# Gate and up products of a two-layer decoder: sixteen of 22 column pairs as seven quadrant products each (Strassen's method), x parked in DRAM meanwhile

## The chip, the cores and the metric

The kernel runs on one core of one Trainium2 chip. The metric is the device time of one execution in microseconds, as the median of three runs. A core has TensorE (PE, matrix products from SBUF into PSUM; the profile shows its weight loads as PEld), VectorE (DVE), ScalarE (ACT), GpSimd (POOL) and SyncE (SP, which issues most of the DMAs here). They run side by side and wait for each other through semaphores.

## The reference, cut to what matters

Two layers of a decoder, for 512 prompt tokens and 32 sample tokens (544 in all). Each layer ends with a gated feed-forward block; D_MODEL = 1024, D_FF = 2816, everything in float32.

```python
h2 = rms_norm(x, g_ffn[l])
gu = h2 @ w_gu[l]
x = x + (jax.nn.silu(gu[..., :D_FF]) * gu[..., D_FF:]) @ w_down[l]
```

Retention and block attention come before this in each layer; the change leaves them as they are.

## The kernel before

**Precision.** A matrix product in float32 is made of three products of rounded parts: each operand has a high part (a ScalarE copy to the type fp32r) and a low part (VectorE: the value minus its high part), and the sum is high x high + high x low + low x high. For weights these parts are WH and WL, for x after the norm's gain XH and XL, for the hidden layer AH and AL. Weights arrive in RAW, two slots of 2048 columns that take turns; each slot is split into WH (`L1072`, ScalarE) and WL (`L1436`, VectorE), and after that SP loads the next but one unit into the slot.

**Layout.** Features lie on the partitions: XT is 8 blocks of 128 features x 544 tokens, and a product's weights (128 x 128) are stationary while 272 tokens (half of 544) move. A *unit* f of the gate and up stage is 128 columns of the gate and the same 128 columns of up, 22 units per layer; a *tile* is one of the two, 8 blocks x 3 parts x 2 halves = 48 matmuls of 272 columns into two banks of PSUM. There are four such pairs of banks, and TensorE takes them in turn.

**One unit.** TensorE: `unit2`, two calls of `feature_tile` (`L637`). VectorE in `gu(i, j)`: multiplies the gate tile by the norm's factor RSTDB (`L1677`), ScalarE makes its sigmoid (`sig`, `L1273`), VectorE multiplies the two (`L1832`), scales the up tile (`L1677`), multiplies (`L1836`); ScalarE stores the high part of the result in AH (`L1335`), VectorE the low part in AL (`L1838`). The factor RSTDB is applied behind the product, so that the product can start before the norm is known.

**Start of the stage.** The first unit follows the output projection's last tile. VectorE adds each block of it to x (`residual`, `L1810`), ScalarE makes XH and the squares. TensorE sums the squares over the partitions (`square_sums`, `L532`), VectorE makes the variance, POOL the power -1/2 (`norm`, `L469`), VectorE puts it on diagonals (`L1382`), TensorE spreads these over all partitions (`spread`, `L542`) between the two tiles of unit 1, and VectorE copies the result into RSTDB (`L1387`, `L1388`). The fourth pair of banks, which unit 1's second tile uses, holds the spread values, so that tile waits for the copies (`rt_taken`).

**The order** is written out by hand: each engine has its own program, and semaphores count tiles (`tile_done`, `tile_free`), split units (`hi_ready`, `lo_ready`) and hidden tiles (`val_ready`, `hi_val`, `x_lo`). `hold` is a wait for a register's value, behind a wait that is always satisfied. After the stage comes the down projection: 8 tiles of 132 matmuls, whose results are added to x (`residual` again), after which the next layer starts.

## Time and profile before

| | us |
|---|---|
| median of 3 runs (lowest, highest) | 2082.14 (2081.86, 2082.91) |
| the profiled execution, its own time | 2080.78 |
| its span, first to last instruction | 2079.2 |
| TensorE busy in the span | 2032.4 |
| VectorE busy | 973.1 |
| ScalarE busy | 685.0 |
| POOL busy | 127.5 |
| mean granted TensorE clock, as a share of full speed | 0.997 |

The profiled execution is one run under the hardware profiler. Busy time is the union of an engine's instructions; matmuls overlap in it (each is shown with 288 ns, though one starts every 125), so their number times their duration says nothing, and the distance between starts does. The chain that ended last is followed back from the last instruction to whatever released it.

### The profile page before, as it was taken

The numbers are of one execution on the slowest core, as the hardware profiler recorded it, in microseconds if no ns is written. First come the engines' busy times: TensorE is split into PE (matmuls) and PEld (weight loads), VectorE is DVE, ScalarE is ACT, GpSimd is POOL, SyncE is SP. The second block draws the span as 40 slices with busy tenths as digits, with TensorE's granted clock in tenths as the row PEclk, the third lists the DMA queues.
The fourth block names the chain that finished last, engine by engine and source line by source line (L and its number), as shares of the span: only waits on it lengthen the run. The fifth ranks groups of instructions, "written<-read, shape, count | busy, mean of one in ns | idle before, by whom it ended". The sixth has DMA issues, their size and how long they took to land.

```text
span 2079.2 us, 45110 instructions
## 1 busy us (share of the span) xinstructions
PE 2032.4 (98%) x17393; PEld 1909.0 (92%) x17393; DVE 973.1 (47%) x1620; ACT 685.0 (33%) x1054; POOL 127.5 (6%) x211
## 2 busy tenths in 40 slices
PE   7989999999999999999999899999999999999999
PEld 6968978989999999999998698799899999999998
...
GB/s 194 123 44 207 214 276 114 86 139 162 120 100 82 83 99 81 82 72 94 96 150 125 65 216 231 273 52 92 198 117 110 106 82 81 83 99 68 84 83 91
DMA packets 257967, 253.20 MB, mean 122 GB/s; under 512 B 12266, under 2 KB 223378, under 8 KB 257554
## 3 DMA queue, kind: packets, MB, share of 16 engines
...
q14 instruction: 62, 0.51, 0.1%
q10 hardware_dynamic: 128, 0.15, 0.0%
...
## 4 chain that ended last, share of the span: by engine, by line
PE 94%; DVE 2%; ACT 2%; issue 1%; DMA 1%; ACTq 0%; POOLq 0%; DVEq 0%; POOL 0%
PE PS L637 62%; PE PS L618 3%; PE PS L793 3%; PE PS L619 3%; PE PS L620 3%; PE PS L598 2%; PE PS L599 2%; PE PS L600 2%; PE PS L804 2%; PE PS L851 1%; PE PS L577 1%; PE PS L733 1%; PE PS L749 1%; ACT PT L1153 1%; PE PS L670 1%
## 5 line engine op out<-in xcount | busy, mean ns | idle before, releaser
L637 PE MATMUL PS<-XH,WH 128*128 128x272 f32 x2176 | 454.6, 290 | 5.1 <-DVE EA L1728 3.2
L637 PE MATMUL PS<-XH,WL 128*128 128x272 f32 x2176 | 450.4, 288 | 0.0
L637 PE MATMUL PS<-XL,WH 128*128 128x272 f32 x2176 | 448.7, 288 | 0.0
L1436 DVE TENSOR_TENSOR WL<-RAW,WH 128x2048 fp32r<-128x2048 f32 (+2 forms) x144 | 310.7, 2157 | 227.1 <-ACT WH L1072 226.3
L637 PEld LDWEIGHTS PS<-XH,WH 128*128 128x128 f32 x2176 | 342.0, 188 | 12.6 <-DVE EA L1728 8.2
L637 PEld LDWEIGHTS PS<-XL,WH 128*128 128x128 f32 x2176 | 341.9, 188 | 0.0
L637 PEld LDWEIGHTS PS<-XH,WL 128*128 128x128 f32 x2176 | 339.9, 189 | 0.0
L1072 ACT ACTIVATE WH<-RAW 128x2048 fp32r<-128x2048 f32 (+2 forms) x152 | 274.5, 1806 | 94.7 <-PE PS L637 87.9
L1677 DVE TENSOR_TENSOR EA<-PS,RSTDB 128x544 f32<-128x544 f32 x120 | 86.3, 721 | 226.5 <-PE PS L637 225.8
L1273 ACT ACTIVATE EB<-EA 128x544 f32<-128x544 f32 x92 | 60.5, 658 | 327.9 <-DVE EA L1677 274.2
L618 PE MATMUL PS<-WH,XH 128*128 128x256 f32 x512 | 153.2, 299 | 0.0
L637 PE MATMUL PS<-AH,WH 128*128 128x272 f32 x704 | 146.1, 289 | 0.0
L619 PE MATMUL PS<-WL,XH 128*128 128x256 f32 x512 | 145.3, 284 | 0.0
L637 PE MATMUL PS<-AL,WH 128*128 128x272 f32 x704 | 145.2, 287 | 0.0
L637 PE MATMUL PS<-AH,WL 128*128 128x272 f32 x704 | 145.0, 287 | 0.0
L620 PE MATMUL PS<-WH,XL 128*128 128x256 f32 x512 | 144.5, 282 | 0.0
L598 PE MATMUL PS<-WH,XH 128*128 128x256 f32 x384 | 110.4, 287 | 8.8 <-DVE WL L1423 6.7
L618 PEld LDWEIGHTS PS<-WH,XH 128*128 128x128 f32 x512 | 97.6, 191 | 21.6 <-ACT RV L1085 12.6
L637 PEld LDWEIGHTS PS<-AL,WH 128*128 128x128 f32 x704 | 111.0, 188 | 0.0
L637 PEld LDWEIGHTS PS<-AH,WL 128*128 128x128 f32 x704 | 109.9, 188 | 0.0
L637 PEld LDWEIGHTS PS<-AH,WH 128*128 128x128 f32 x704 | 109.9, 188 | 0.0
L599 PE MATMUL PS<-WL,XH 128*128 128x256 f32 x384 | 109.4, 285 | 0.0
...
## 6 DMA issues: line engine op xcount, KB each, us to landing
...
```

The source lines that it names most:

```text
L598: pe.matmul(out, a, wh[:, k], start=k == 0, stop=False)
L599: pe.matmul(out, a, wl[:, k], start=False, stop=False)
L600: last = pe.matmul(out, b, wh[:, k], start=False, stop=k == KT - 1)
L618: pe.matmul(out, a, wh[:, k], start=k == 0, stop=False)
L619: pe.matmul(out, a, wl[:, k], start=False, stop=False)
L620: last = pe.matmul(out, b, wh[:, k], start=False, stop=k == KT - 1)
L637: last = pe.matmul(PS[:, 2 * pair + h, 0:HALF], w[:, i, c0:c0 + P], x[:, k, h * HALF:(h + 1) * HALF], start=first and i == 0 and a == 0, s ...
L793: last = pe.transpose(PS[:, (c + 2) % 3, hp * P:(hp + 1) * P], buf[:, b, hp * P:(hp + 1) * P], IDENT)
L1072: act.activation(WH[:, slot, 0:n], RAW[:, slot, 0:n], ACT.Copy).then_inc(hi_ready, 1)
L1273: act.activation(EB[:, dst, :], EA[:, src, :], ACT.Sigmoid).then_inc(sig_done, 1)
L1436: dve.tensor_tensor(WL[:, slot, 0:n], RAW[:, slot, 0:n], WH[:, slot, 0:n].bitcast(F32), ALU.subtract).then_inc(lo_ready, 1)
L1677: dve.tensor_tensor(halves(dst), pair[p], RB, ALU.mult).then_inc(tile_free, 1)
```

## The change

**The quadrants.** For units 6 to 21 (NC = 6), x after norm and gain (8 blocks x 544 tokens) is cut into four quadrants of 4 blocks x 272 tokens, and a unit's weights into four quadrants of 4 blocks x 128 columns: 11 and 21 are the two halves of the gate's blocks, 12 and 22 those of up. The product of two 2 x 2 matrices is then made of seven products of quadrants (or of sums of them) in place of eight. A quadrant product is 4 blocks x 3 parts = 12 matmuls of 272 columns.

**x.** ScalarE writes x times its gain into XF (8 operations), VectorE multiplies it by RSTDB, makes four sums of quadrants (SF), and the two split the four sums and three plain quadrants (Q11, QS1, QS2, Q12, QS3, QS4, Q22) into high and low parts. QS1 and QS2 lie where XT is, so POOL first stores XT to DRAM (`x_parked`, 2.2 MB) and loads it back after the last unit. Q12, QS3, QS4 and Q22 lie where XH and XL are, which units 0 to 5 read.

**The weights.** RAW's slot holds four quadrants, from four DMAs of 256 KB in place of two of 512 KB. For each unit the three quadrants 11, 21 and 22 are split as they are (`a_high`, `a_low`, 1536 columns), VectorE makes four sums in place (`w_sums`, 512 columns each, each waiting for the one before), and four sums are split in two pairs (`t12_*`, `t34_*`, 1024 columns each). The parts lie in CH, over WH and WL.

**The products.** Three PSUM banks per unit, two sets for odd and even units. The first product goes into bank a; ScalarE copies it to bank c, where the fourth is added; the second goes to bank f and is copied to one more bank; third, fifth and seventh are added to a, the sixth to f, and ScalarE copies a twice to SBUF in between. One extra matmul marks bank c as written, so that the fourth product adds to ScalarE's copy. VectorE's `up_sum`, `gate_mul` and `gated_up` make the hidden tile, and the bank set is free after `gate_mul`.

**Other parts.** `spread` is moved from behind unit 1's first tile to behind its fifth block of eight. The hidden layer's last blocks lie in a tail. A wait for x's return is added to the down projection's residual.

```diff
+    QUAD = 8 * HK * HALF
+    Q11 = quadrant_pair("Q11", TAILOFF)
+    QS1, QS2 = quadrant_pair("QS1", 16512), quadrant_pair("QS2", 16512 + QUAD)
+    Q12, QS3, QS4, Q22 = (quadrant_pair(n, XHOFF + i * QUAD) for i, n in enumerate(("Q12", "QS3", "QS4", "Q22")))
+    XF = at("XF", [P, KT, N], F32, R0 + 12 * N * 4)
...
+    XTF = nc.dram_tensor("x_parked", [P, KT, N], F32)
...
+            hold(pool, x_lo, lay * NX + X0["out"] + KT)
+            hold(pool, xg_done, lay + 1)
+            pool.dma_start(XTF.ap(), XT[:]).then_inc(xf_kept, 16)
             norm(2 * lay + 2)
+            hold(pool, tile_done, lay * NT + T0["down"])
+            hold(pool, xf_kept, lay * 16 + 16)
+            pool.dma_start(XT[:], XTF.ap()).then_inc(xf_back, 16)
...
-            feature_tile(T0["gu"] + 2, 2, 1, UC, 0, kk, x)
+            feature_tile(T0["gu"] + 2, 2, 1, UC, 0, kk, x, final=False, part=kk[:5])
             spread(2 * lay + 2, (6, 7))
+            feature_tile(T0["gu"] + 2, 2, 1, UC, 0, kk, x, first=False, part=kk[5:])
...
+            def seven(f, j):
+                at_c, s = w_chunks(j), f - NC
+                c_bank, a_bank, f_bank = 4 * j, 4 * j + 1, 4 * j + 2
+                a_hi, a_lo = CH[:, a_slots(j, 0)], CH[:, a_slots(j, 1)]
+                t1, t2 = (0, 1) if j else (1, 0)
...
+                def product(q, w, bank, n, start=False):
+                    if isinstance(f, int) and f == NC:
+                        pe.wait_ge(q_lo, lay * 7 + n)
+                    wh, wl = (v.rearrange("p (k c) -> p k c", c=P) for v in w)
+                    for k in range(HK):
+                        for m, (a, b) in enumerate(((wh, q[0]), (wh, q[1]), (wl, q[0]))):
+                            last = pe.matmul(PS[:, bank, 0:HALF], a[:, k, :], b[:, k, :],
+                                             start=start and k == m == 0, stop=k == HK - 1 and m == 2,
+                                             skip_group_check=not start)
+                    return last
+                def copies(n):
+                    pe.wait_ge(copied, lay * (4 * NSU) + 4 * s + n)
+                pe.wait_ge(la_ready, lay * NSU + s + 1)
+                pe.wait_ge(tile_free, lay * NT + 2 * f + T0["gu"])
+                if isinstance(f, int) and f == NC:
+                    pe.wait_ge(q_lo, lay * 7 + 1)
+                pe.matmul(PS[:, c_bank, 0:HALF], a_hi[:, at_c["11"] - 1, 0:P], Q11[0][:, 0, :], start=True, stop=True)
+                product(Q11, a_chunk("11"), a_bank, 1, start=True).then_inc(prod, 1)
+                pe.wait_ge(l12_ready, lay * NSU + s + 1)
+                product(QS1, t_chunk(t12, t1), f_bank, 2, start=True).then_inc(prod, 1)
+                copies(1)
+                product(QS2, t_chunk(t12, t2), a_bank, 3).then_inc(prod, 1)
+                product(Q12, a_chunk("21"), c_bank, 4).then_inc(prod, 1)
+                pe.wait_ge(lo_ready, lay * NU + f + (U0["gu"] + 3))
+                copies(3)
+                product(QS3, t_chunk(t34, 0), a_bank, 5).then_inc(prod, 1)
+                product(QS4, a_chunk("22"), f_bank, 6).then_inc(prod, 1)
+                copies(4)
+                product(Q22, t_chunk(t34, 1), a_bank, 7).then_inc(tile_done, 2)
+            seven(NC, 0)
+            seven(NC + 1, 1)
+            with pe.Fori(NC // 2 + 1, FT // 2) as i:
+                for j in range(2):
+                    seven(2 * i + j, j)
...
+            def a_high(f, j):
+                s = f - NC
+                hold(act, landed[j], (lay * NU + U0["gu"] + f) * 16 + (32 - 16 * j))
+                hold(act, landed_up[j], (lay * NSU + s) * 16 + (32 - 16 * j))
+                if isinstance(f, int) and f == NC:
+                    unit_done(NC - 2)
+                else:
+                    act.wait_ge(prod, lay * (6 * NSU) + 6 * (s - 1) + 1)
+                act.activation(CH[:, a_slots(j, 0)], raw_chunks(j)[:, 1:4], ACT.Copy).then_inc(ha_ready, 1)
...
+            def seven(f, j):
+                b = 4 * j
+                first = isinstance(f, int) and f == NC
+                if first:
+                    unit_done(NC - 1)
+                    quad_hi(4, Q12, x_quad(XF, 1, 0))
+                    quad_hi(5, QS3, SF[:, 2])
+                else:
+                    gate_high(f - 1, 1 - j)
+                    t34_high(f, j)
+                copy(f, PS[:, b, 0:HALF], b + 1, 1)
+                if first:
+                    quad_hi(6, QS4, SF[:, 3])
+                    quad_hi(7, Q22, x_quad(XF, 1, 1))
+                elif isinstance(f, int) and f == FT - 1:
+                    split(U0["down"], 0, 11 * P, (prod, lay * (6 * NSU) + 6 * (f - NC) + 1))
+                else:
+                    a_high(f + 1, 1 - j)
+                copy(f, PS[:, b + 3, 0:HALF], b + 2, 2)
+                if not first:
+                    hidden_high(f - 1)
+                copy(f, EB[:, 1, 0:HALF], b + 1, 3)
+                if first:
+                    sig(T0["gu"] + 2 * (NC - 1), 0, 0, 0)
+                copy(f, EB[:, 1, HALF:N], b + 1, 5)
+                if first:
+                    hidden_high(NC - 1)
+                    a_high(f + 1, 1 - j)
+                if not (isinstance(f, int) and f == FT - 1):
+                    t12_high(f + 1, 1 - j)
...
             ahead("gu", 0, 0, 2)
+            for k in range(KT):
+                xg = act.activation(XF[:, k, :], XT[:, k, :], ACT.Copy,
+                                    scale=GT[:, bass.ds(8 * lay + (k + 16), 1)])
+            xg.then_inc(xg_done, 1)
             ahead("gu", 0, 1, 2)
             gu(0, 0)
+            ahead("gu", 1, 0, 2)
             gu(0, 1)
-            with act.Fori(1, FT // 2) as i:
+            quad_hi(1, Q11, x_quad(XF, 0, 0))
+            ahead("gu", 1, 1, 2)
+            gu(1, 0)
+            act.wait_ge(xf_kept, lay * 16 + 16)
+            quad_hi(2, QS1, SF[:, 0])
+            ahead("gu", 2, 0, 2)
+            gu(1, 1)
+            quad_hi(3, QS2, SF[:, 1])
+            a_high(NC, 0)
+            gu(2, 0)
+            t12_high(NC, 0)
+            t34_high(NC, 0)
+            seven(NC, 0)
...
+            def quad_low(n, q, src):
+                dve.wait_ge(q_hi, lay * 7 + n)
+                dve.tensor_tensor(q[1][:], src, q[0][:].bitcast(F32), ALU.subtract).then_inc(q_lo, 1)
+            def a_low(f, j):
+                dve.wait_ge(ha_ready, lay * NSU + (f - NC) + 1)
+                dve.tensor_tensor(CH[:, a_slots(j, 1)], raw_chunks(j)[:, 1:4], CH[:, a_slots(j, 0)].bitcast(F32),
+                                  ALU.subtract).then_inc(la_ready, 1)
+            def w_sums(f, j):
+                r, c, n = raw_chunks(j), w_chunks(j), lay * (4 * NSU) + 4 * (f - NC)
+                b11, b12, b21, b22 = (r[:, c[q], :] for q in ("11", "12", "21", "22"))
+                dve.wait_ge(la_ready, lay * NSU + (f - NC) + 1)
+                dve.tensor_tensor(b11, b11, b12, ALU.subtract).then_inc(w_sum, 1)
+                dve.wait_ge(w_sum, n + 1)
+                dve.tensor_tensor(b12, b22, b12, ALU.subtract).then_inc(w_sum, 1)
+                dve.wait_ge(w_sum, n + 2)
+                dve.tensor_tensor(b22, b22, b11, ALU.add).then_inc(w_sum, 1)
+                dve.wait_ge(w_sum, n + 3)
+                dve.tensor_tensor(b21, b21, b22, ALU.subtract).then_inc(w_sum, 1)
+            def t12_low(f, j):
+                dve.wait_ge(h12_ready, lay * NSU + (f - NC) + 1)
+                dve.tensor_tensor(t12(f, 1), raw_t12(j), t12(f, 0).bitcast(F32), ALU.subtract).then_inc(l12_ready, 1)
+            def t34_low(f, j):
+                dve.wait_ge(hi_ready, lay * NU + f + (U0["gu"] + 1))
+                dve.tensor_tensor(t34(f, 1), raw_t34(j), t34(f, 0).bitcast(F32), ALU.subtract).then_inc(lo_ready, 1)
+            def up_sum(f, j):
+                s = f - NC
+                dve.wait_ge(prod, lay * (6 * NSU) + 6 * s + 6)
+                dve.wait_ge(copied, lay * (4 * NSU) + 4 * s + 4)
+                if isinstance(f, int) and f == FT - 1:
+                    dve.wait_ge(x_lo, lay * NX + X0["gu"] + f)
+                dve.tensor_tensor(halves(EA[:, 1, :]), halves(EB[:, 1, :]), pair[2 * j + 1], ALU.subtract)
+            def gate_mul(f, j):
+                dve.wait_ge(sig_done, lay * NSIG + f + (S0N["gu"] + 1))
+                dve.tensor_tensor(halves(EB[:, 0, :]), pair[2 * j], halves(EB[:, 0, :]), ALU.mult).then_inc(tile_free, 2)
+            def gated_up(f):
+                dve.wait_ge(tile_free, lay * NT + 2 * f + (T0["gu"] + 4))
+                dve.tensor_tensor(EA[:, 1, :], EA[:, 1, :], EB[:, 0, :], ALU.mult).then_inc(val_ready, 1)
+            def seven(f, j):
+                last = isinstance(f, int) and f == FT - 1
+                up_sum(f - 1, 1 - j)
+                gate_mul(f - 1, 1 - j)
+                t34_low(f, j)
+                gated_up(f - 1)
+                if last:
+                    split(U0["down"], 0, 11 * P)
+                else:
+                    a_low(f + 1, 1 - j)
+                hidden_low(f - 1)
+                if not last:
+                    w_sums(f + 1, 1 - j)
+                    t12_low(f + 1, 1 - j)
...
+            split(U0["gu"] + 1, 1, 8 * UC)
             variance(2 * lay + 2, 6)
             spread_rt(2 * lay + 2)
-            ahead("gu", 0, 1)
+            split(U0["gu"] + 2, 0, 8 * UC)
             take_rt(2 * lay + 2, (6, 7))
             dve.wait_ge(rt_taken, 2 * lay + 2)
-            gu(0, 0)
-            gu(0, 1)
-            hold(dve, tile_free, lay * NT + T0["gu"] + 4)
-            with own.loop(FT // 2 - 1, 2) as i:
+            gu(0)
+            dve.wait_ge(xg_done, lay + 1)
+            dve.tensor_tensor(XF[:], XF[:], RSTDB[:].unsqueeze(1).to_broadcast([P, KT, N]), ALU.mult)\
+                .then_inc(xf_ready, 1)
+            split(U0["gu"] + 3, 1, 8 * UC)
+            gu(1)
+            dve.wait_ge(xf_ready, lay + 1)
+            quad_sum(SF[:, 0], xa(1, 0), xa(1, 1), ALU.add)
+            quad_sum(SF[:, 2], xa(0, 0), xa(1, 0), ALU.subtract)
+            dve.wait_ge(sf_ready, lay * 4 + 1)
+            quad_sum(SF[:, 1], SF[:, 0], xa(0, 0), ALU.subtract)
+            quad_low(1, Q11, xa(0, 0))
+            split(U0["gu"] + 4, 0, 8 * UC)
+            gu(2)
+            dve.wait_ge(sf_ready, lay * 4 + 3)
+            quad_sum(SF[:, 3], SF[:, 1], xa(0, 1), ALU.subtract)
+            quad_low(2, QS1, SF[:, 0])
+            split(U0["gu"] + 5, 1, 8 * UC)
+            gu(3)
+            quad_low(3, QS2, SF[:, 1])
+            a_low(NC, 0)
+            gu(4)
+            w_sums(NC, 0)
+            t12_low(NC, 0)
+            t34_low(NC, 0)
+            quad_low(4, Q12, xa(0, 1))
+            quad_low(5, QS3, SF[:, 2])
+            quad_low(6, QS4, SF[:, 3])
+            quad_low(7, Q22, xa(1, 1))
+            gu(NC - 1)
+            a_low(NC + 1, 1)
+            w_sums(NC + 1, 1)
+            t12_low(NC + 1, 1)
+            seven(NC + 1, 1)
```

**How the order of instructions moves.** VectorE in the loop over the units, register rows left out: before, one unit (EA and EB are the scaled tiles in SBUF, PS is PSUM):

```order
L1436 TENSOR_TENSOR WL<-RAW,WH 128x2048
L1677 TENSOR_TENSOR EA<-PS,RSTDB 128x544
L1832 TENSOR_TENSOR EB<-EB,EA 128x544
L1677 TENSOR_TENSOR EA<-PS,RSTDB 128x544
L1836 TENSOR_TENSOR EA<-EA,EB 128x544
L1838 TENSOR_TENSOR AL<-EA,AH 128x544
```

and after the change, one unit (RAW<-RAW are the four sums; CH<- the low parts of the weights; T34H holds the high parts of T3 and T4):

```order
L2124 TENSOR_TENSOR EA<-EB,PS 128x544
L2128 TENSOR_TENSOR EB<-PS,EB 128x544
L2115 TENSOR_TENSOR CH<-RAW,T34H 128x2x512
L2132 TENSOR_TENSOR EA<-EA,EB 128x544
L2093 TENSOR_TENSOR CH<-RAW,CH 128x1536
L2082 TENSOR_TENSOR AL<-EA,AH 128x544
L2101 TENSOR_TENSOR RAW<-RAW 128x512
L2103 TENSOR_TENSOR RAW<-RAW 128x512
L2105 TENSOR_TENSOR RAW<-RAW 128x512
L2107 TENSOR_TENSOR RAW<-RAW 128x512
L2111 TENSOR_TENSOR CH<-RAW,CH 128x1024
```

The two scalings by RSTDB and the split of 2048 columns are gone; in their place there are two operations on PSUM, low parts of 1024, 1536 and 1024 columns and four sums of 512.

VectorE between unit 5 and unit 7 (units 6's low parts, four quadrants of x, all of unit 5, and the low part of unit 7's plain quadrants):

```order
L2115 TENSOR_TENSOR FIRST34L<-RAW,FIRST34H 128x1024
L2089 TENSOR_TENSOR Q12L<-XF,Q12H 128x1088
L2089 TENSOR_TENSOR QS3L<-SF,QS3H 128x1088
L2089 TENSOR_TENSOR QS4L<-SF,QS4H 128x1088
L2089 TENSOR_TENSOR Q22L<-XF,Q22H 128x1088
L1917 TENSOR_TENSOR EA<-PS,RSTDB 128x544
L2069 TENSOR_TENSOR EB<-EB,EA 128x544
L1917 TENSOR_TENSOR EA<-PS,RSTDB 128x544
L2073 TENSOR_TENSOR EA<-EA,EB 128x544
L2082 TENSOR_TENSOR AL<-EA,AH 128x544
L2093 TENSOR_TENSOR CH<-RAW,CH 128x1536
```

The four low parts of x stand ahead of unit 5's products with PSUM, and `CH<-RAW,CH 128x1536`, which unit 7's first product waits for, behind all of them.

TensorE around the spread in unit 1 (EA holds the diagonals, REGISTER_ALU prepares the wait at the head of a tile), before: the last rows of the unit's first tile, the spread, the head of its second:

```order
L637 MATMUL PS<-XH,WH 128x272 x2
L637 MATMUL PS<-XL,WH 128x272 x2
L637 MATMUL PS<-XH,WL 128x272 x2
L542 MATMUL PS<-EA,FIX 128x128 x4
L543 MATMUL PS<-EA,FIX 128x32
L631 REGISTER_ALU
L637 MATMUL PS<-XH,WH 128x272 x2
L637 MATMUL PS<-XL,WH 128x272 x2
L637 MATMUL PS<-XH,WL 128x272 x2
L637 MATMUL PS<-XH,WH 128x272 x2
```

and after the change, from the spread on:

```order
L623 MATMUL PS<-EA,FIX 128x128 x4
L624 MATMUL PS<-EA,FIX 128x32
L719 MATMUL PS<-XH,WH 128x272 x2
L719 MATMUL PS<-XL,WH 128x272 x2
L719 MATMUL PS<-XH,WL 128x272 x2
L719 MATMUL PS<-XH,WH 128x272 x2
L719 MATMUL PS<-XL,WH 128x272 x2
L719 MATMUL PS<-XH,WL 128x272 x2
L719 MATMUL PS<-XH,WH 128x272 x2
L719 MATMUL PS<-XL,WH 128x272 x2
L719 MATMUL PS<-XH,WL 128x272 x2
L712 REGISTER_ALU
```

Nine rows of the first tile, 18 matmuls, now stand behind the spread and ahead of the second tile.

## Rows read from the trace of the kernel before

**Rows 1.** The page: busy time by engine, and the chain by engine.
```profile
PE 2032.4 (98%) x17393; PEld 1909.0 (92%) x17393; DVE 973.1 (47%) x1620; ACT 685.0 (33%) x1054; POOL 127.5 (6%) x211
...
PE 94%; DVE 2%; ACT 2%; issue 1%; DMA 1%; ACTq 0%; POOLq 0%; DVEq 0%; POOL 0%
```

**Rows 2.** The chain in order of time, one entry (start, us, what).
```profile
664.66 379.43 PE PS L637 x3024
```

**Rows 3.** Timeline of one gate and up unit: start us, us, engine, operation.
```profile
759.33 2.29 DVE L1436 TENSOR_TENSOR WL<-RAW,WH 128x2048 fp32r<-128x2048 f32 x1 [0.96 <-ACT WH L1072]
...
759.97 0.41 PE L637 MATMUL PS<-XH,WL 128*128 128x272 f32 x2
...
760.22 0.41 PE L637 MATMUL PS<-XH,WH 128*128 128x272 f32 x2
...
761.54 0.72 DVE L1677 TENSOR_TENSOR EA<-PS,RSTDB 128x544 f32<-128x544 f32 x1
...
762.29 0.66 ACT L1273 ACTIVATE EB<-EA 128x544 f32<-128x544 f32 x1 [2.99 <-DVE EA L1677]
...
767.19 0.72 DVE L1677 TENSOR_TENSOR EA<-PS,RSTDB 128x544 f32<-128x544 f32 x1 [3.48 <-PE PS L637]
...
767.95 0.72 DVE L1836 TENSOR_TENSOR EA<-EA,EB 128x544 f32<-128x544 f32 x1
...
768.87 0.66 ACT L1335 ACTIVATE AH<-EA 128x544 f32 x1 [5.92 <-DVE EA L1836]
```

**Rows 4.** Timeline at the start and the end of the gate and up stage.
```profile
643.10 0.41 PE L637 MATMUL PS<-XH,WH 128*128 128x272 f32 x2
...
655.33 1.91 ACT L1072 ACTIVATE WH<-RAW 128x2048 fp32r<-128x2048 f32 x1 [7.73 <-PE PS L637]
...
656.63 1.20 POOL L469 TENSOR_TENSOR SM<-SM 128x5 f32<-128x5 f32 x1 [56.41 <-DVE SM L1377]
...
662.32 0.94 PE L542 MATMUL PS<-EA,FIX 128*128 128x128 f32 x7
...
911.31 0.41 PE L637 MATMUL PS<-AH,WH 128*128 128x272 f32 x2
```

**Rows 5.** Timeline: TensorE behind a wait that ended late, in the gate stage.
```profile
460.73 0.52 PE L637 MATMUL PS<-XH,WH 128*128 128x272 f32 x2 [0.51 <-DVE EA L1728]
```

**Rows 6.** VectorE by form: names, shapes, count | busy us, mean ns | idle before.
```profile
L1436 DVE TENSOR_TENSOR WL<-RAW,WH 128x2048 fp32r<-128x2048 f32 x120 | 274.9, 2291 | 220.0 <-ACT WH L1072 220.0
...
L1442 DVE TENSOR_TENSOR WL<-RAW,WH 128x1024 fp32r<-128x1024 f32 x16 | 19.5, 1221 | 15.0 <-ACT WH L1072 15.0
...
L1795 DVE TENSOR_TENSOR G<-G,EA 128x544 f32 x12 | 8.7, 726 | 2.8 <-DVE EA L1791 2.8
...
L1648 DVE TENSOR_TENSOR RK<-RK,CL 128x512 f32<-128x512 f32 x8 | 5.0, 684 | 0.0
```

**Rows 7.** ScalarE by form, the same columns.
```profile
L1072 ACT ACTIVATE WH<-RAW 128x2048 fp32r<-128x2048 f32 x128 | 244.3, 1908 | 94.7 <-PE PS L637 87.9 <-DMA RAW<-in_w_in 6.7
...
L1040 ACT ACTIVATE XH<-XT,GT x32 | 24.0, 751 | 181.4 <-DVE XT L1810 181.4
...
L1072 ACT ACTIVATE WH<-RAW 128x1024 fp32r<-128x1024 f32 x8 | 8.4, 1051 | 0.0
...
L1153 ACT ACTIVATE PT<-PS 128x256 f32<-128x256 f32 x8 | 3.1, 384 | 5.2 <-PE PS L733 5.2
```

**Rows 8.** The weight DMA's line, 700 to 900 us: duration ns min/median/max; landing.
```profile
L382 SPq DMA_DIRECT2D RAW<-in_w_gu x30: 372/383/396, 701.8 to 870.7; - x30
...
DMA to landing us min/median/max: 3.1/4.0/5.1
```

**Rows 9.** DMA issues of the whole span: KB each, median us to landing.
```profile
x_kept<-XT SPq DMA_DIRECT2D x2, 2048.0 KB, 10.9
```

**Rows 10.** Two windows: busy us of each engine, granted clock, DMA share, GB/s.
```profile
20.00:30.00 10.00, 6.11 (x41) 6.09 (x42) 6.25 (x12) 8.33 (x11) 0.00 (x0) 0.66 0.09 15
1040.00:1050.00 10.00, 7.97 (x71) 7.73 (x71) 2.20 (x4) 1.30 (x2) 0.00 (x0) 1.00 0.47 138
```

140 lines of the change are left out of this document (122 added, 18 removed).

## The prediction

> **What bounds the kernel now.** The page's first part says that TensorE is busy for 98% of the span, and the chain that ended last is TensorE for 94% [rows 1]. Both only say where to look, since a busy TensorE may still wait inside a stage. The chain in order of time settles it for this stage: one stretch of 3024 matmuls without another engine in it, 379.43 us, from the second tile of unit 1 through the gate and up products and all of the down projection [rows 2]. That is 0.1255 us per matmul, tile boundaries and loop branches included. So here a matmul that is removed is worth its pitch, as long as nothing else becomes late. The timeline of one unit shows the pitch and how idle the others are: two matmuls every 0.25 us, while VectorE has six operations and ScalarE three in a unit of 12.03 us (the greater part of them in [rows 3]). From the first matmul of the stage to the first of the down projection it is 911.31 - 643.10 = 268.2 us [rows 4], and twice that in the program.
>
> **TensorE's part.** A unit (128 gate and 128 up columns) costs 2 tiles x 8 x 3 x 2 = 96 matmuls of 272 columns. Unit 2 starts at 664.66 + 48 x 0.1254 = 670.68, and twenty units later it is 911.31: 12.03 us each [rows 2, 4]. As seven products it is 7 x 4 x 3 = 84 and one that only marks a bank: 85, of the same width and with one weight load each, as before. 12.03 x 85/96 = 10.65, plus 0.01 for each of seven boundaries (the 0.1255 above against 0.1253 inside a tile, over 48 matmuls): 10.72 us, 1.31 less. Sixteen units give **-21.0 us** per layer. Bounds: no boundary cost, 10.65; or a restart at every product as after the wait at 460.73, whose pair took 0.52 in place of 0.41 [rows 5], 7 x 0.11 more, 11.4. I take the low side, since the wait of that row came late and these come long before.
>
> The Trainium skill (TensorE: Matmul & The Clock Gate, section on the back-to-back issue gap) gives columns/2.4 + 2.5 ns for a lone stream, 116 ns for 272 columns. By it the eleven matmuls are worth 1.27 us a unit and not 1.38; the rows say 125, and the measurement decides.
>
> **Does VectorE keep up?** Its chain for one unit in the new loop, with durations from [rows 3, 6]: two operations on PSUM 2 x 0.72, low part of T3/T4 (1024) 1.22, product 0.72, low part of the three plain quadrants (1536, between 1024 and 2048) 1.76, low part of the hidden tile 0.72, four sums of 512 at 0.68, low part of T1/T2 1.22: 9.8 us. An independent operation starts 0.08 before the one ahead ends (759.33 + 2.29 against 761.54), one that waits for its predecessor 0.04 after (767.19 + 0.72 against 767.95) [rows 3]; seven of the first and three of the second, -0.4. After the third sum ScalarE needs 1.05 for the high part, of which the fourth sum covers 0.7: +0.4. About **9.8 to 9.9 us per unit against 10.72**: VectorE goes from half busy to 90%, but does not bound. ScalarE: 0.66 sigmoid, 1.05, 1.48, 1.05 for the splits, 0.66 hidden, four copies of 272 at 0.40 = 6.5 us [rows 3, 7].
>
> Where in the unit are the waits (t = 0 its first matmul)? Product 1 ends at 1.6, and then every 1.5. ScalarE sees the unit before finished at 0.2, sigmoid to 0.9, T3/T4 high to 1.8, first copy about 2.2; product 3 needs it at 3.1. VectorE: gate product 0.9 to 1.6, T3/T4 low to 3.1; product 5 needs it at 6.2. T1/T2 low of the next unit is finished at 9.8 to 10, needed at 12.3. Slack everywhere is 0.9 us or more, so the steady loop should run at TensorE's pace. The landing: a slot of RAW is free at 3.1, now four issues of 0.38 and about 4.0 to land (5.1 at most) [rows 8], so 5.5 to 6.7; ScalarE reads it 9.9 us after it was free. 3 us of cover.
>
> **The first six units.** New beside them: on ScalarE eight products of 0.75 [rows 7] (in a hole of 7.7 us before 655.33 [rows 4]), three high parts of 1088; on VectorE 4352 elements (4.7 by the same slope), four sums and three low parts of 1088 at 1.29. A unit's own work is 2.29 + 5 x 0.72 = 5.9 us of VectorE and leaves 6.1: the new 13.7 us fit into the 30 of five units, and counted through in order the low parts of the weights of units 3, 4 and 5 are still finished 7 us before TensorE asks. Zero; if the cover went, at most the 4.7 would show once. POOL has the store of x ahead of its power for the norm: a DMA issue took 0.38 on SP [rows 8], and ScalarE is done at about 653, 3.6 us before the power starts at 656.63 [rows 4]. Zero, or 1 at most.
> **Spread moved.** Tile 2 of unit 1 now has its last 18 matmuls (2.3 us) behind the broadcast of the norm. Now TensorE waits from the broadcast at 662.32, which takes about 1.2, until 664.66 [rows 2, 4]: **-1.1 us**.
>
> **The change of regime, units 6 and 7.** Here I expect the loss. T=0 is unit 6's start. Four quadrants of x live where XH and XL were, so their low parts can only follow unit 5: VectorE has T3/T4 low until 2.3, four low parts of 1.29 until 7.2, and only then unit 5's own five operations with ScalarE's two between (7.1 to 10.7). ScalarE makes unit 5's hidden high part until 11.5 and, behind it in its queue, the high part of unit 7's quadrants until 12.9; VectorE's low part ends at 14.7. TensorE could have started unit 7 at 10.85 and starts at 14.8: **+4.0**. Then three sums (2.2), ScalarE 1.05, VectorE 1.22: 19.3, where product 2 wants it at 16.4: **+2.9**. Product 3 of unit 6 waits 0.1 for its copy. Bounds: 6.5 if every handover is as short as 0.03 (762.29 behind 761.54 + 0.72), 8.5 if each is the 0.20 of 768.87 behind 767.95 + 0.72 [rows 3].
> **The end.** The old loop freed each bank pair in the unit's middle; now both are freed together after the sigmoid, and the first down tile asks for that: 0.2 + 0.66 + 0.72 and handovers, **+1.8** (bounds 1.6 and 2.1). Today there is nothing there: 911.31 follows the last gate matmul. The way back of x (2.2 MB; a 2 MB store took 10.9 [rows 9], so some 12 to 14 us with the issue) is asked for 18 us later, by the first residual: hidden.
>
> **Sum per layer:** -21.0 - 1.1 + 7.0 + 1.8 = -13.3; twice, -26.7. The profiled execution took 2080.78 us around a span of 2079.2; the median of the three is 2082.14, 1.36 more. 2080.8 - 26.7 = 2054.1, and on the median's scale **2055 us**.
>
> **Rivals.**
> *A, the clock falls after the stall.* TensorE is idle 4.0 us, works 1.6, is idle 2.9. With 2.0 of 10 us not busy the granted clock stayed at 1.00 from 1040 to 1050; with 3.9 of 10 it was 0.66 from 20 to 30, so partly at 1.2 and partly at 2.4 GHz [rows 10]. Around unit 7 it is 6.9 in some 10 us. Price: 0.34 of 10 us is 3.4 us lost, so up to 3.4 per layer: 2062. The Trainium skill (TensorE: Matmul & The Clock Gate, section on why this matters) states that an idle gap between bursts throttles the engine again; by this rule A is what happens. The rows agree for the longer pause and not for the short one.
> *B, VectorE sets the pace mildly.* If half of its junctions cost more than I gave them, the chain is 11.2 us and not 9.9. Then 14 units lose 0.45 each: +6.3 per layer, 2068. For: 90% load and no run of such a chain in the trace. Against: 0.85 us of margin.
> *C, slower.* One mechanism: the waits in VectorE's chain. Where a hold on its own semaphore stood before the sum of L1795 it was idle for 2.8/12 = 0.23 us [rows 6]. Eleven such junctions in each unit make 9.8 + 2.5 = 12.4 us. From 11.7 on the sixteen units are no gain (13.3/14 = 0.95 above 10.72); at 12.4 it is +1.7 x 14 - 13.3 = +10 per layer, **2102 us**. Against it: the chain's waits are of the kind of L1836 (0.04), without the hold.
> *D, the change doesn't do what it says.* Every product restarts TensorE (11.4 us a unit, above): 0.7 x 16 = 11 per layer come back, 2078, a gain that can hardly be measured.
>
> **Numbers.** Forecast 0.60; A 0.14; B 0.16; C 0.05; D 0.05. Forecast's own bounds: 2055 less 2 (boundaries), less 1 (short handovers) and plus 3 (long ones), 2052 to 2058. A and B take the top to 2068, and below I leave 3 more, since unit 7's loss is a sum of fourteen steps that may overlap more than I see: 2049 to 2068, which leaves out C, D and the upper part of B. A measurement of this kernel can tell 0.2%, 4 us, from no change. Faster by more: forecast, A, B and half of D, 0.92; within: 0.03; slower: 0.05.
>
> **What would show it.** In the new profile: units of unit 8 on 10.7 us apart, with no idle time of TensorE inside; VectorE at 90% in that stretch and its waits for TensorE and the sigmoid still there (if they are gone, B or C); TensorE idle near 4 and 3 us at the first and second product of unit 7 and 1.8 before the first down matmul; granted clock behind unit 7 (A); first pairs of products at 0.41 and not 0.52 (D). The forecast is wrong if the steady period is above 11, or if unit 7 loses less than 5 or more than 9 us.

## Result and the profile of the changed kernel

The changed kernel takes **2056.88 us** (median of 4 runs, 2053.70 to 2059.82) against 2082.0 us before (4 runs beside it): ratio 0.9879, 95% interval 0.9862 to 0.9896. The forecast was 2055 us, in the range 2049 to 2068. The profiled execution took 2053.70 us around a span of 2052.1, 27.1 less than the 2079.2 of before; the sum of the prediction said 26.7.

The page's first part, busy time and instructions of each engine, answers to [rows 1]:

```profile
PE 1996.7 (97%) x17041; PEld 1870.4 (91%) x17041; DVE 1124.9 (55%) x1804; ACT 805.8 (39%) x1276; POOL 130.8 (6%) x215
```

TensorE has 352 matmuls and 35.7 us of busy time less; the span lost only 27. The chain of layer 1 and the same marks of layer 2, in order of time (start, length, what), answers to [rows 2, 4]. An entry that follows another without a wait begins where that one ends:

```profile
654.71 0.79 PE PS L613 x8
...
655.67 3.97 PE PS L719 x30
...
660.86 44.46 PE PS L719 x354
...
728.10 1.48 ACT CH L1490
729.61 1.77 DVE CH L2093
...
733.57 1.07 ACT CH L1498
734.66 1.23 DVE CH L2111
735.94 9.35 PE PS L1114 x72
745.29 0.12 PE PS L1126
745.42 10.56 PE PS L1114 x84
...
756.10 10.57 PE PS L1114 x84
...
766.79 10.57 PE PS L1114 x84
...
884.42 10.58 PE PS L1114 x84
...
895.03 0.63 ACT EB L1515
...
895.75 0.73 DVE EB L2128
...
896.53 132.37 PE PS L719 x1056
...
1666.96 44.46 PE PS L719 x354
...
1742.05 10.69 PE PS L1114 x72
...
1903.98 132.39 PE PS L719 x1056
```

Where before one stretch of TensorE ran through, there is now a piece of ScalarE and VectorE at unit 7 (728 to 736), then unit after unit at 10.69 us (884.42 - 745.42 = 139.00 for thirteen), then 1.53 us without a matmul before down (896.53 - 884.42 - 10.58), in which ScalarE makes unit 21's sigmoid and VectorE its `gate_mul`.

A matmul is shown with 0.29 us although the next one starts after 0.125. So what a wait costs is read from starts. From the timeline of TensorE (start, length, what): the first matmul of units 6, 7 and 8, the last of unit 21, the first of down:

```profile
717.14 0.29 PE L1126 MATMUL PS<-Q11H,CH 128*128 128x272 f32 x1
...
731.49 0.59 PE L1126 MATMUL PS<-Q11H,CH 128*128 128x272 f32 x1 [3.53 <-DVE CH L2093]
...
745.13 0.29 PE L1126 MATMUL PS<-Q11H,CH 128*128 128x272 f32 x1
...
894.70 0.29 PE L1114 MATMUL PS<-Q22H,CH 128*128 128x272 f32 x1
...
896.53 0.51 PE L719 MATMUL PS<-AH,WH 128*128 128x272 f32 x2 [1.54 <-DVE EB L2128]
```

Units 6 and 7 took 745.13 - 717.14 = 27.99 us, 6.6 more than two of 10.69. The first matmul of down started 1.83 us after the last of unit 21, so the junction cost 1.7. What TensorE waits for, over the whole program (us in total, times, longest):

```profile
PE PS L1126 <- DVE CH L2093: 7.1, 2, 3.5
...
PE PS L719 <- DVE EB L2128: 3.1, 2, 1.5
PE PS L1114 <- DVE CH L2111: 2.8, 2, 1.7
```

The columns of the next view are busy time (with the number of instructions) of TensorE, of its weight loads, VectorE, ScalarE and POOL, then granted clock, DMA share and GB/s. Three stretches: layer 1's unit 7, the steady units of layer 1, layer 2's unit 7:

```profile
728.00:732.00 4.00, 0.51 (x2) 0.51 (x3) 3.09 (x3) 1.57 (x2) 0.00 (x0) 0.92 0.00 0
732.00:736.00 4.00, 2.86 (x14) 2.54 (x12) 3.50 (x6) 2.43 (x4) 0.00 (x0) 0.65 0.00 0
736.00:740.00 4.00, 4.00 (x32) 4.00 (x33) 4.00 (x5) 3.09 (x6) 0.00 (x0) 1.00 0.04 13
...
745.00:884.00 139.00, 139.00 (x1107) 139.00 (x1106) 124.25 (x145) 80.27 (x117) 0.00 (x0) 1.00 0.33 96
...
1736.00:1740.00 4.00, 2.40 (x13) 2.41 (x13) 3.86 (x5) 0.32 (x1) 0.00 (x0) 0.79 0.00 0
1740.00:1744.00 4.00, 2.30 (x10) 1.98 (x10) 3.60 (x5) 3.88 (x5) 0.00 (x0) 0.50 0.00 0
1744.00:1748.00 4.00, 4.00 (x30) 4.00 (x29) 3.97 (x6) 1.35 (x3) 0.00 (x0) 0.86 0.52 152
```

In the steady stretch TensorE is never idle and VectorE is busy 89%. What VectorE still waits for there, in one unit of its timeline, is ScalarE, four times and 1.05 us together:

```profile
797.32 1.23 DVE L2111 TENSOR_TENSOR CH<-RAW,CH 128x1024 fp32r<-128x1024 f32 x1 [0.40 <-ACT CH L1498]
...
799.52 0.72 DVE L2128 TENSOR_TENSOR EB<-PS,EB 128x544 f32<-128x544 f32 x1 [0.35 <-ACT EB L1515]
800.40 1.23 DVE L2115 TENSOR_TENSOR CH<-RAW,T34H 128x1024 fp32r<-128x1024 f32 x1 [0.15 <-ACT T34H L1506]
...
802.41 1.76 DVE L2093 TENSOR_TENSOR CH<-RAW,CH 128x1536 fp32r<-128x1536 f32 x1 [0.15 <-ACT CH L1490]
```

At unit 7 the clock falls in both layers, in layer 1 only while product 1 runs, in layer 2 until 1744 and later. The chain shows what that costs: the same 72 matmuls take 9.35 us in layer 1 and 10.69 in layer 2.

**A measure for the experiments.** From the first matmul behind the spread to the first of down it is 896.53 - 660.86 = 235.67 us in layer 1 and 1903.98 - 1666.96 = 237.02 in layer 2. Where the clock holds, such "stage times" come again to 0.01 us in other kernels of the same order, while the run times scatter by 5 us and more; so what a few us mean is read from them. (What comes before the stage ends at different times in the profiles, 653.5 to 657.5; the kernel before, at 655.3, lies among them.)

### The profile page after: what moved, and what is told of

The parts are those of the page before. It is cut to its first block, busy times and chain, and to the rows that moved or that the text cites. A ratio compares the mean times of both kernels' runs of the same rounds, so it can differ in the third digit from the quotient of the medians.

```text
span 2052.1 us, 45522 instructions
## 1 busy us (share of the span) xinstructions
PE 1996.7 (97%) x17041; PEld 1870.4 (91%) x17041; DVE 1124.9 (55%) x1804; ACT 805.8 (39%) x1276; POOL 130.8 (6%) x215
## 4 chain that ended last, share of the span: by engine, by line
PE 90%; DVE 4%; ACT 3%; issue 2%; DMA 1%; ACTq 0%; DVEq 0%; POOLq 0%; POOL 0%
PE PS L719 43%; PE PS L1114 15%; PE PS L699 3%; PE PS L700 3%; PE PS L701 3%; PE PS L875 3%; PE PS L679 2%; PE PS L680 2%; PE PS L681 2%; PE PS L933 2%; PE PS L886 1%; PE PS L658 1%; PE PS L815 1%; PE PS L831 1%; ACT PT L1287 1%
## 5 line engine op out<-in xcount | busy, mean ns | idle before, releaser
L1676 DVE TENSOR_TENSOR WL<-RAW,WH 128x2048 fp32r<-128x2048 f32 (+2 forms) x112 | 236.0, 2107 | 198.5 <-ACT WH L1206 197.6
L1206 ACT ACTIVATE WH<-RAW 128x2048 fp32r<-128x2048 f32 (+2 forms) x120 | 212.5, 1771 | 106.0 <-PE PS L719 95.4
L719 PE MATMUL PS<-XH,WH 128*128 128x272 f32 x1152 | 243.1, 292 | 3.2 <-DVE EA L1968 3.2
L719 PE MATMUL PS<-XL,WH 128*128 128x272 f32 x1152 | 237.9, 288 | 0.0
L719 PE MATMUL PS<-XH,WL 128*128 128x272 f32 x1152 | 237.7, 288 | 0.0
L719 PEld LDWEIGHTS PS<-XH,WH 128*128 128x128 f32 x1152 | 180.6, 188 | 10.6 <-DVE EA L1968 8.2
L719 PEld LDWEIGHTS PS<-XL,WH 128*128 128x128 f32 x1152 | 181.0, 188 | 0.0
L719 PEld LDWEIGHTS PS<-XH,WL 128*128 128x128 f32 x1152 | 180.3, 189 | 0.0
L701 PE MATMUL PS<-WH,XL 128*128 128x256 f32 x512 | 144.1, 281 | 0.0
L1407 ACT ACTIVATE EB<-EA 128x544 f32<-128x544 f32 x60 | 39.5, 660 | 228.2 <-DVE EA L1917 174.4
L699 PEld LDWEIGHTS PS<-WH,XH 128*128 128x128 f32 x512 | 97.1, 190 | 21.6 <-ACT RV L1219 11.7
L681 PE MATMUL PS<-WH,XL 128*128 128x256 f32 x384 | 109.3, 285 | 0.0
```

The source lines that it names most:

```text
L681: last = pe.matmul(out, b, wh[:, k], start=False, stop=k == KT - 1)
L699: pe.matmul(out, a, wh[:, k], start=k == 0, stop=False)
L701: last = pe.matmul(out, b, wh[:, k], start=False, stop=k == KT - 1)
L719: last = pe.matmul(PS[:, 2 * pair + h, 0:HALF], w[:, i, c0:c0 + P], block[:, h * HALF:(h + 1) * HALF], start=first and i == 0 and a == 0, ...
L1206: act.activation(WH[:, slot, 0:n], RAW[:, slot, 0:n], ACT.Copy).then_inc(hi_ready, 1)
L1676: dve.tensor_tensor(WL[:, slot, 0:n], RAW[:, slot, 0:n], WH[:, slot, 0:n].bitcast(F32), ALU.subtract).then_inc(lo_ready, 1)
```

## Experiments

Ten kernels, and the changed one again, in three groups; each group ran on one chip beside the kernel before. Ratios are to the kernel before.

**1. TensorE kept busy in unit 7's waits.**

```diff
...
+                if isinstance(f, int) and f == NC + 1:
+                    pe.wait_ge(tile_free, lay * NT + 2 * f + T0["gu"])
+                idle_work(26)
                 pe.wait_ge(la_ready, lay * NSU + s + 1)
...
                 product(Q11, a_chunk("11"), a_bank, 1, start=True).then_inc(prod, 1)
+                idle_work(20)
```

> The changed kernel, with 26 and then 20 matmuls whose result nobody reads, issued by TensorE into the free bank 7 where it waits at unit 7 (before its product 1 and before its product 2). Nothing of the result is left out. My theory: both waits stay where they are, since VectorE ends them; TensorE only looks busy in them. What changes is the clock behind them: in the changed kernel's trace the last 72 products of unit 7 took 9.35 us in layer 1 and 10.69 us in layer 2, against 72 x 125.3 ns = 9.02 us at full clock. With the clock kept at 1.00 this gives back 0.33 + 1.67 = 2.0 us of the profiled run, and more in the runs that lay up to 6 us over it: the median should come to 2052 to 2054 us, and the four to six runs should lie within 2 us of one another in place of 6. The rival (the scatter has nothing to do with unit 7's clock) expects the same scatter and a time of 2055 to 2059 us. A second rival: the added matmuls end too late and delay product 1, then the time rises by up to 2 us for both layers.

2052.84 us (4 runs, 2049.83 to 2054.92), ratio 0.9856 (0.9841 to 0.9871). The stage takes 235.67 us in both layers, and the 72 matmuls behind the wait 9.34 in both. The windows over the same place as above:

```profile
728.00:732.00 4.00, 4.00 (x34) 4.00 (x33) 2.53 (x4) 2.04 (x2) 0.00 (x0) 1.00 0.00 0
732.00:736.00 4.00, 3.81 (x31) 3.59 (x30) 3.60 (x5) 0.96 (x1) 0.00 (x0) 1.00 0.00 0
736.00:740.00 4.00, 3.86 (x31) 3.64 (x30) 3.86 (x5) 3.61 (x6) 0.00 (x0) 1.00 0.01 4
```

VectorE is no earlier, so nothing but the clock changed: its fall cost 0 in layer 1 and 1.35 us in layer 2 of the changed kernel's profile, not 2.0. My expectation had counted 72 x 125.3 ns = 9.02 us; they take 9.34 at full clock too, since the entry counts the last matmul to its end (0.16) and the first behind a wait takes 0.1 longer. The fall costs nothing where it is over by the end of product 1, since product 2 waits for VectorE anyway. The granted clock over the whole run rose to 0.997 to 0.999. The scatter of 5 us did not shrink to the 2 us I had expected, so unit 7's clock is not what makes most of it.

**2. Without the matmul that marks bank c.**

```diff
-                pe.matmul(PS[:, c_bank, 0:HALF], a_hi[:, at_c["11"] - 1, 0:P], Q11[0][:, 0, :], start=True, stop=True)
```

> The changed kernel without the one matmul per unit whose result product 2 overwrites. What is computed stays the same. If TensorE alone sets the pace of the sixteen units, each becomes shorter by one matmul, 10.69 to 10.56 us, and the time falls by 32 x 0.125 = 4.0 us (2052 to 2054 us). The rival, that VectorE's chain (9.8 us of work in 10.69) or the slots it frees set the pace in part, expects less than half of that, 0 to -2 us, and idle time of TensorE inside the units.

(The matmul's result is overwritten by ScalarE's copy, not by product 2 as the expectation says.) 2050.14 us (5 runs, 2047.35 to 2052.65), ratio 0.9845 (0.9832 to 0.9859). Layer 1's stage takes 233.94 us, 1.73 less: that is 14 matmuls of 0.125, those of units 8 to 21. Those of units 6 and 7 are worth nothing, since there TensorE only comes earlier to a wait that VectorE ends. In layer 2 the clock fell for longer, and the stage took 235.91. So TensorE alone sets the pace of the steady units. (Why the fourth product needs no mark to add to ScalarE's copy here, no run shows.)

**3, 4. Three, and one, more VectorE operations per unit.**

```diff
                 gated_up(f - 1)
+                for i in range(3):
+                    dve.tensor_reduce(SM[:, 76 + 2 * i:78 + 2 * i] if i < 2 else SM[:, 90:92], PADSRC, AX, ALU.max)
```

> The changed kernel with three operations of VectorE more in each of the units 7 to 21: each reduces 512 elements of a constant to two numbers that nobody reads. Each should take 0.55 to 0.75 us, so VectorE's work rises from 8.9 us busy of a 10.69 us unit to about 10.8 us, over the pace of TensorE with the waits between the operations (9.8 us with them before). My theory (VectorE has about 0.9 us of room) expects the unit at 10.69 + 0.6 to 1.6 us, 11.3 to 12.3 us, TensorE waiting within each unit, and 15 x 2 x that = +18 to +48 us. If a wait of TensorE in each unit also pulls the clock down, products take up to twice as long and the time rises far more, by over 100 us. If VectorE had more room than I thought (its waits shrink by what is added), the rise is below 10 us.

Three: 2075.45 us (6 runs, 2073.33 to 2077.47), ratio 0.9971 (0.9959 to 0.9983). The stage takes 247.27 us, 11.60 more, which is 0.83 for each of fourteen units: 11.52 us per unit. Twelve units of it, first by group of instructions (busy us, mean ns | idle before, releaser), then as a window:

```profile
L2144 DVE TENSOR_REDUCE SM<-FIX 128x2 f32<-128x512 f32 x36 | 22.4, 677 | 0.0
L1114 PE MATMUL PS<-QS1H,CH 128*128 128x272 f32 x96 | 21.3, 302 | 6.7 <-DVE CH L2111 6.7
L1114 PEld LDWEIGHTS PS<-QS1H,CH 128*128 128x128 f32 x96 | 15.8, 188 | 9.4 <-DVE CH L2111 9.4
```

```profile
753.00:891.00 138.00, 131.26 (x1021) 128.62 (x1020) 131.97 (x169) 70.83 (x108) 0.00 (x0) 1.00 0.32 91
```

The chain shows VectorE's three operations as 1.78 us on the path of every unit, and TensorE waits once in each, at product 2, for the low part of T1 and T2. VectorE's own timeline has only one wait left in a unit, the 0.40 us for ScalarE. So VectorE needs 11.52 - 1.78 = 9.74 us for a unit without them: 0.95 of room. The wait of each unit, 0.56 us of matmuls and 0.78 of weight loads (6.7 and 9.4 in twelve units), did not lower the clock: it is 1.00 in the window.

> The changed kernel with one operation of VectorE more in each of the units 7 to 21, of 0.60 us (three of them took 1.78 us in the kernel with three, whose units became 11.52 us long, 0.83 us over TensorE's pace). By the same count one of them leaves VectorE's chain at 11.52 - 1.19 = 10.33 us, under TensorE's 10.69: the unit stays at 10.69 us, its only cost is at unit 7, where VectorE is already late, so 2 x 0.6 us at most, +1 us. The rival, that every addition of VectorE's is paid in part even under the pace (a third of 0.6 us per unit), expects +6 us.

One: 2054.47 us (4 runs, 2048.73 to 2056.69), ratio 0.9868 (0.9849 to 0.9886). The stage takes 235.66 us in both layers, unchanged to 0.01. VectorE under TensorE's pace costs nothing (9.74 + 0.59 against 10.69); over it, the excess is paid in full.

**5. x parked twice.**

```diff
             pool.dma_start(XTF.ap(), XT[:]).then_inc(xf_kept, 16)
+            pool.dma_start(XTF2.ap(), XT[:]).then_inc(xf_kept, 16)
...
-            hold(pool, xf_kept, lay * 16 + 16)
+            hold(pool, xf_kept, lay * 32 + 32)
             pool.dma_start(XT[:], XTF.ap()).then_inc(xf_back, 16)
+            hold(pool, xf_back, lay * 32 + 16)
+            pool.dma_start(XT[:], XTF2.ap()).then_inc(xf_back, 16)
```

> The changed kernel with x stored to DRAM twice and brought back twice, one after the other: 2176 KB more each way and layer, the second store holding back ScalarE's first write to the place of x, the second load the first addition of x at the down tiles. My theory prices the parking at nothing: the store takes 7.6 us from issue to landing and is over long before QS1 is written, the way back is hidden behind the wait for the first down tile. Twice as much should then cost 0 to 1 us per layer, 0 to 2 us in all; the second load ends some 8 to 10 us later than the first, which still lies within the first two down tiles (2 x 2.75 us do not quite hold it), so VectorE's first addition may be late by up to 4 us, and TensorE has four banks of slack before it waits. The rival, that the parking takes bandwidth from the weight loads of the first units or holds back ScalarE, expects +3 us or more, the same amount that the parking itself costs now.

2054.93 us (4 runs, 2053.01 to 2057.85), ratio 0.9872 (0.9857 to 0.9887): no dearer than once. The second way back was late for VectorE in one layer, and TensorE, with its banks ahead, had no wait for it:

```profile
DVE XT L2054 <- DMA XT<-x_parked: 5.8, 1, 5.8
```

Layer 2's stage is 235.67 us. Layer 1's is 237.79, where the 72 matmuls of unit 7 took 11.45 us, 2.11 more than at full clock: again the clock and nothing else. The parking is free, and a transfer twice as long would be.

**6. The order before unit 7 changed** (VectorE; ScalarE's queue is changed to match).

```diff
+            scaled(tile, 2, EA[:, 0, :])
+            a_low(NC + 1, 1)
             quad_low(6, QS4, SF[:, 3])
+            dve.wait_ge(sig_done, lay * NSIG + g + (S0N["gu"] + 1))
+            own.mark(dve.tensor_tensor(EB[:, 0, :], EB[:, 0, :], EA[:, 0, :], ALU.mult))
             quad_low(7, Q22, xa(1, 1))
-            gu(NC - 1)
-            a_low(NC + 1, 1)
+            scaled(tile + 1, 3, EA[:, 1, :])
...
             w_sums(NC + 1, 1)
+            hidden_low(g)
             t12_low(NC + 1, 1)
```

> The changed kernel with VectorE's and ScalarE's work before unit 7 in another order: the residues and high parts of unit 7's own weights (a_high, a_low) are taken before the last two quadrants' (quad_hi and quad_low 6 and 7), and these are put between the steps of unit 5's gate. Nothing is left out. In the changed kernel TensorE waits 3.5 us before unit 7's product 1 for VectorE's a_low and 1.2 to 1.7 us before product 2 for t12_low, with product 1 at the half clock between them: 28 matmuls in 2 to 3 us less or more. Stepping through the order with the measured durations, a_low is ready before TensorE comes, so the first wait goes and what is left of the second is 1 to 2 us; unit 8 starts about 3 us earlier in each layer: -6 us, 2050 to 2051 us. The clock should then also fall less behind it. The rival (VectorE is late as a whole, its work before unit 8 cannot be moved but only added up) expects that the wait moves to product 2 or to unit 8 with the same length, and the time stays within 1 us of the changed kernel's.

2048.91 us (5 runs, 2045.48 to 2049.82), ratio 0.9841 (0.9828 to 0.9855). TensorE's waits in layer 1 from 700 to 760:

```profile
PE PS L1114 <- DVE CH L2111: 2.5, 1, 2.5
```

The wait before product 1 is gone, the one before product 2 is 2.5 us, and the stage takes 232.62 us, 3.05 less. VectorE now works without a pause from 717.8 to 733.9, so what is left is its amount of work and not its order. In layer 2 the clock fell behind the one wait too: 234.13, 1.51 more.

**7. The first down tile waits for its own bank only.** `feature_tile` begins with `pe.wait_ge(tile_free, lay * NT + tile + 3 - depth)`.

```diff
                         last = feature_tile(tile, m, j, P, 0, range(11 * j, 11 * j + 11), (HIDDEN_HI, HIDDEN_LO), j == 0, j == 1,
-                                            depth=2)
+                                            depth=4 if isinstance(i, int) and m == 0 else 2)
```

> The changed kernel, whose first down tile takes its chunks with a look-ahead of four matmul groups in place of two, so that TensorE reaches the last hidden chunk (k = 21, the one that unit 21's gate gives) later within its tile. Nothing is left out. TensorE waits 1.5 us at the start of down for the unit 21's sigmoid and VectorE's product in both layers. My theory: the wait is for work that ends about 1.5 us after unit 21's last product, so doing as much other work first hides it: -1.5 us a layer, -3 us in all (2053 to 2054 us). The rival: the wait is not for the hidden chunk but for a bank that VectorE's gate_mul frees, then the look-ahead changes nothing and the 1.5 us stay.

2054.46 us (4 runs, 2050.42 to 2054.92), ratio 0.9865 (0.9850 to 0.9880). The wait is gone: down begins at once behind unit 21.

```profile
887.64 10.57 PE PS L1114 x84
898.21 16.89 PE PS L719 x135
```

(For this the first round of the loop over the down tiles is written out, which the diff above does not show.) The expectation reads `depth` as a look-ahead over the chunks, and the order of the matmuls is in fact the same as before. `depth` says how many tiles back the bank must have been freed. With 2, the first down tile waits for `gate_mul` of unit 21; with 4, for that of unit 20. Unit 20 is the last that used the banks 0 and 1, into which this tile writes; unit 21 lies in 4 to 7. So the run shows the very thing that the expectation's rival names: the wait was for a freed bank, as the prediction has it, and for the bank of the wrong unit.

In this profile the clock cost 2.28 and 1.98 us at unit 7 (72 matmuls in 11.62 and 11.32 us), so the stage reads 236.41 and 236.09: without it 234.1, which is 235.67 - 1.53. (By starts the gain is 1.7, since the entry at 898.21 begins 0.17 after its first matmul.) Read from the run times alone the edit would have looked like nothing.

**8. Only the spread moved, in the kernel before.**

```diff
-            feature_tile(T0["gu"] + 2, 2, 1, UC, 0, kk, x)
+            feature_tile(T0["gu"] + 2, 2, 1, UC, 0, kk, x, final=False, part=kk[:5])
             spread(2 * lay + 2, (6, 7))
+            feature_tile(T0["gu"] + 2, 2, 1, UC, 0, kk, x, first=False, part=kk[5:])
```

> The kernel before, with only the place of the spread (the two small products that turn the root-mean-square into a row of factors) moved as in the change: before the last three chunks of unit 0's third tile in place of behind it. The parts of the change that make seven products of eight are not in it. My theory: VectorE's copy of the factors then runs beside the three chunks' matmuls, the wait of 1.3 us behind the spread goes, and each layer becomes 1.1 us shorter: -2.2 us against the kernel before, 2079 to 2080.5 us. The rival, that the gate's first use of the factors is the one that is waited for, expects no change.

2078.01 us (11 runs, 2075.35 to 2080.64), ratio 0.9983 (0.9974 to 0.9992). From the sums of squares to the entry behind the spread the chain has 660.15 - 654.00 = 6.15 us; before it was 664.66 - 655.29 = 9.37, in which TensorE did 18 matmuls more (2.26 us). That is 0.96 us per layer, and 1.03 by the starts of the matmuls. It is not all that the edit gave. From the first square sum to the first matmul of down, by the timelines:

```profile
655.13 0.95 PE L532 MATMUL PS<-FIX,EB 128*128 128x1 f32 x8
...
911.31 0.41 PE L637 MATMUL PS<-AH,WH 128*128 128x272 f32 x2
```

```profile
653.84 0.83 PE L532 MATMUL PS<-FIX,EB 128*128 128x1 f32 x7
...
908.43 0.41 PE L637 MATMUL PS<-AH,WH 128*128 128x272 f32 x2
```

256.18 us before, 254.59 in this kernel: 1.59 less per layer, 3.2 in the program, well inside the interval (0.8 to 2.6 per thousand, 1.7 to 5.4 us). The other 0.55 are spread over the stage: a unit takes 12.00 us and not 12.03, and no run shows why. In the changed kernel units 2 to 5 take 12.00 us too. The 1.0 us per layer of the spread, and the 0.1 of these first units, have nothing to do with the seven products.

**9. The three gains together, without and with filling the wait; and the changed kernel again.**

> The changed kernel with the new order before unit 7, the deeper look-ahead of the first down tile, and without the matmul that marks bank c. From the first matmul behind the spread to the first of down, the profiles without a fall of the clock took 235.67 us; the order alone took 232.62 (-3.05), the look-ahead ended unit 21 and began down without the 1.53 us between them, the mark's absence gave 233.94 (-1.73). If the three add up, this stage takes 229.4 us where the clock holds and up to 2 us more where it falls behind the 2.5 us wait before unit 7's product 2; the time is 2 x 6.3 = 12.6 us under the 2052.8 us of the kernel whose clock held, plus 0 to 4: 2040 to 2044 us. If the gains overlap (unit 7's wait grows by what TensorE saves before it), up to 1 us per layer less is gained.

> As the run before it, with 20 matmuls in the wait before unit 7's product 2, into bank 7, whose result nobody reads. Nothing of the result is left out. My theory: the wait stays 2.5 us long, the clock holds behind it, the stage takes 229.4 us in both layers, and the time comes to 2040 us, 0 to 4 us under the kernel without them. The rival (the fall of the clock comes and goes with something other than this wait) expects the same time for both.

> The changed kernel as it is, once more, on the same chip as the two before it. My theory: the stage takes 235.67 us plus what the clock costs behind unit 7's two waits, 0, 1.35 or 2.12 us in the four layers seen so far, each run its own; the runs lie between 2052 and 2060 us with a granted clock of 0.990 to 0.997, and those with the higher clock are the shorter ones. The rival, that the clock has no part in the scatter, expects the long runs to have the same clock as the short ones.

| kernel | us (runs) | ratio, 95% interval | stage, layers 1 and 2 | granted clock of the runs |
|---|---|---|---|---|
| order, own bank, no mark | 2041.08 (5) | 0.9809 (0.9796 to 0.9823) | 229.35, 230.86 | 0.996 to 0.998 |
| the same, wait filled | 2041.45 (5) | 0.9801 (0.9788 to 0.9815) | 229.35, 229.35 | 0.997 to 0.999 |
| changed kernel again | 2054.85 (4) | 0.9867 (0.9851 to 0.9882) | 235.66, 237.16 | 0.994 to 0.998 |

The rows are, in this order, the kernel with the new order before unit 7, the first down tile's wait and no mark; the same with 20 unread matmuls in the wait before product 2; the changed kernel. The three gains add up to 0.01 us: 235.67 - 3.05 - 1.53 - 1.73 = 229.36. The kernel with all three is 13.8 us faster than the changed one on the same chip and 40 us faster than the one before. Filling the wait held the clock in both layers (worth 1.51 us in layer 2), but the run times don't show it. The changed kernel's runs of both groups, time and clock: 2051.45 at 0.998, 2052.92 at 0.996, 2053.70 at 0.995, 2056.11 at 0.993, 2056.78 at 0.995, 2057.31 at 0.994, 2057.65 at 0.994, 2059.82 at 0.990. The longer runs have the lower clock, with small exceptions. The kernels with the 3.5 us wait filled or gone (experiments 1, 6 and the two of 9) had no run under 0.996, the lowest of the changed kernel's eight being 0.990. That the clock makes the runs longer by as much is not shown: the scatter of 5 us stayed when it was held at unit 7.

## Why the prediction was right, step by step

- **Sixteen units.** Forecast 10.72 us each, -21.0 per layer; measured 10.69, so 16 x (12.03 - 10.69) = -21.4. The boundaries of the products cost 0.04 us together (10.69 - 10.65), half of what I gave them. From the rule of the Trainium skill for an isolated matmul (TensorE: Matmul & The Clock Gate, section on the back-to-back issue gap) the estimate for the eleven matmuls is 1.27 us; 1.34 were gained.
- **VectorE keeps up.** Forecast 9.8 to 9.9 us per unit; 9.74 by the kernel with three more operations. In the steady unit it still waits for the sigmoid (0.35 us), which itself waits for TensorE; TensorE has no wait. Rival B (11.2 us) and rival C (12.4, slower than before) fall with that. VectorE's waits for itself, which stand between the four sums, cost 0.03 us each (794.05, 794.77, 795.50, at 0.69 long) and not the 0.23 of [rows 6]. The threshold behind C (no gain from 11.7 us on) fits: at 11.52 us the ratio was 0.9971.
- **The spread.** Forecast -1.1, measured -1.0, alone and within the change.
- **Units 6 and 7.** Forecast +7.0, measured **+6.6** (27.99 - 2 x 10.69). The parts were less exact: 3.5 us and not 4.0 before product 1; product 1, partly at half clock, took 3.3 us in layer 1 (731.49 to 734.80) and not 1.6; and so only 1.1 to 1.7 before product 2 in this profile and not 2.9. The sum holds since VectorE's chain sets when product 2 starts, whatever TensorE does before it: 735.94 - 717.14 = 18.8 us after unit 6, forecast 19.3.
- **The end.** Forecast +1.8, measured +1.7, within my bounds of 1.6 and 2.1, and for the reason given: the bank that is freed after the sigmoid. But I took this wait for a price of the seven products. The first down tile has no need of that bank, and one number in its wait took the whole term away (experiment 7).
- **First six units, POOL's store, x's way back.** Forecast zero; the first wait of TensorE in the stage is that of unit 7, and twice the parking cost nothing.
- **Sum.** By these rows -21.4 - 1.0 + 6.6 + 1.7 = -14.1 per layer. From the sums of squares to down it was 911.31 - 655.29 = 256.02 us and is 896.53 - 654.71 = 241.82, which is -14.2; forecast -13.3. (The last 0.1 lies in the units 1 to 5, see experiment 8.) Of the 0.9 us per layer by which the sum was too cautious, 0.4 are of the units, 0.4 of unit 7, 0.1 of the end.
- **Luck in the total.** Layer 2 has the clock's 1.35 on top, so 2 x 14.2 - 1.35 = 27.05, and the spans differ by 27.1. That forecast (26.7) and measurement are so close is in part luck. The caution of 2 x 0.9 and the missing 1.35 of the clock have opposite signs. And the rest of the program came out equal to 0.1 us only in this pair of profiles: in the second profile of the same kernel it took 3 us longer (span 2055.2, stage times 235.66 and 237.16).
- **Rival A.** It happened, in part and beside the forecast, which I had set up as one or the other. The clock falls in every layer of the changed kernel's two profiles; behind product 1 it cost 0 to 1.5 us in a layer there, 2.3 at most in its variants, and not up to 3.4. The Trainium skill (TensorE: Matmul & The Clock Gate, section on why this matters) says that an idle gap throttles the engine again, and the windows above agree (0.65 in layer 1, 0.50 in layer 2). I had read the two windows of [rows 10] as a choice between all of it and nothing, and a part belonged into the sum: it was the one missing term that makes the kernel slower, and the median of 2056.88, 1.9 over the forecast, is in keeping with it; that was not measured apart.
- **Rival D.** Falls: no restart at the products of the steady units, at 10.69 us each.
